# Where SBUF tiles lie: the same program with other start addresses

## The chip, the cores and the metric

The kernel runs on one core of a Trainium2 chip. The metric is the device time of one execution in microseconds. The kernel before was run three times: 2685.95, 2686.35 and 2686.78 us, median 2686.35.

## The reference

One layer over 2048 tokens of width 1024, float32. Both token mixers read the same normalised input, sigmoid gates merge them, and a two-level mixture of experts follows:

```
h    = rms_norm(x, g1)
qa, ka, va, qb, kb, vb, gates = split(h @ w_in)
ya   = swa_sink_attention(qa, ka, va)      # 8 query, 2 key heads, bands of 128 keys, bias, sinks
yb   = stick_breaking_attention(qb, kb, vb)  # 8 heads, strictly causal
       # A[t,s] = sig(z_ts) * prod_{s<j<t} (1 - sig(z_tj))
gate = sigmoid(gates + b_gate)
x    = x + (gate[0] * (ya @ w_proj_a) + gate[1] * (yb @ w_proj_b)) @ w_out
h2   = rms_norm(x, g2)
x    = x + moe(h2)   # top-1 of 4 groups, top-2 of its 8 experts: (silu(h2 @ w1) * (h2 @ w3)) @ w2
```

## The kernel before, in words

The program is written engine by engine; five functions run one after the other, each with its own SBUF tiles, and all engines meet at the end of each.

- `norm_and_values` (tiles nt_, 0 to 125 us): normalises and turns the rows, and makes the values of the second attention.
- `projection_and_banded_attention` (ip_, bb_, ba_, 125 to 520 us): the other projections, with the banded attention's steps set between them.
- `stick_breaking_and_gates` (sb_, 520 to 1284 us): 320 units of 128 query rows by up to 512 keys. For each unit TensorE makes the scores sb_z (two matmuls, L1097 and L1100), ScalarE two sigmoids (L945, L946), VectorE a running product into one of four rows of sb_R (L1018), GpSimd the product of sb_sig and sb_R (L1078). TensorE turns this into sb_pst (L1107), ScalarE and VectorE split it into sb_aT_hi and sb_aT_lo (L958, L1026), and TensorE multiplies with the values (L1124). The gate projections (sb_psg) are laid between by a fixed table of pace.
- `merge_and_output_projection` (mo_, 1284 to 1716 us): both attention projections, gates, output projection, second norm, logits.
- `routing_and_experts` (rt_, ex_, from 1716 us): the routing, a chain of small VectorE steps, then blocks of 128 rows. SP loads each expert's weights in pieces of 512 KB into ex_w; ScalarE rounds a piece (L1787, L1794), VectorE subtracts to get the rest (L1939, L1944).

Every float32 product is made of three passes over a rounded part and a rest, `_hi` and `_lo` (`passes3`, L50 to L54), so nearly all of TensorE's work stands on lines 52 to 54.

Tiles are taken with `nc.sbuf_tensor` under an `ExitStack`. The place that a tile gets within each partition follows from the order of these calls: each one takes the next free bytes, rounded up to a multiple of 32, above what is still held, and a function's tiles are given back when it ends. sb_R, [128, 4, 1025] float32, is 16400 bytes in a partition and is rounded up to 16416, the only large tile of its function that is no multiple of 64 bytes.

Of the kernel before, what the change touches and what calls it, by code (L numbers as in the profile page):

```python
# [18 lines left out]
I32 = mybir.dt.int32  # L19
# [4 lines left out]
P = 128  # L24
# [14 lines left out]
NE = 32  # L39
# [4 lines left out]
MAXB = 2 * S // P + NE  # L44
# [25 lines left out]
def norm_and_values(nc, x, g, ident_d, wv_d, hT_hi, hT_lo, vhl, stage, next_tiles, next_in, stored):  # L70

    with ExitStack() as c:
        sb = lambda n, s, d=F32: c.enter_context(nc.sbuf_tensor(n, s, d))
# [9 lines left out]
        junk = sb("nt_sq", [P, D], BF16)  # L83
        g_bc = sb("nt_g", [P, D])
        ident = sb("nt_ident", [P, P])
        wv = sb("nt_wv", [P, 2, 2, TC])
        wv_hi, wv_lo = sb("nt_wv_hi", [P, KD, TC], F32R), sb("nt_wv_lo", [P, KD, TC], F32R)
        vo = sb("nt_vo", [P, 2, HB, 2, HD], F32R)
        ssq, rms = sb("nt_ssq", [P, 2]), sb("nt_rms", [P, 2])
        eps, rstd = sb("nt_eps", [P, 1]), sb("nt_rstd", [P, 2])  # L90
        pt = c.enter_context(nc.psum_tensor("nt_ps", [P, 2, KD, P], F32))
        pv = c.enter_context(nc.psum_tensor("nt_pv", [P, 2, HB, HD], F32))
        g_in, ident_in = sem("nt_g_in"), sem("nt_ident_in")
# [167 lines left out]
def projection_and_banded_attention(nc, w_tiles, hT_hi, hT_lo, projF, qk_hi, qk_lo, hT_d, table, onehot, bias_z,  # L261
# [6 lines left out]
    KW = P + CHUNK  # L268
# [8 lines left out]
    with ExitStack() as c:  # L277
        sb = lambda n, s, d=F32: c.enter_context(nc.sbuf_tensor(n, s, d))
# [13 lines left out]
        tab_hi, pair = sb("bb_hi", [2 * NB, 8], F32R), sb("bb_pair", [2 * NB, 8], F32R)  # L292
        oh = sb("bb_onehot", [2 * NB, ZP], F32R)
        line = sb("bb_line", [8, ZP])
        sink = sb("ba_sink", [P, 2, 4])
        gq, gk = sb("ba_gq", [P, 1]), sb("ba_gk", [P, 1])
        eps, mx = sb("ba_eps", [P, 1]), sb("ba_mx", [P, 8])
        q = sb("ba_q", [P, 2, 4, P])
        k = sb("ba_k", [P, 2, KW])
        v = sb("ba_v", [P, 2, KW])  # L300
        qsq, rq, lnq = sb("ba_qsq", [P, 4, P]), sb("ba_rq", [P, 4, P]), sb("ba_lnq", [P, 4, P])
        kn, rk, ksq, lnk = sb("ba_kn", [P, KW]), sb("ba_rk", [P, KW]), sb("ba_ksq", [P, KW]), sb("ba_lnk", [P, KW])
        qn, vn = sb("ba_qn", [P, 2, 4, CHUNK]), sb("ba_vn", [P, 2, 2, P])
# [444 lines left out]
def stick_breaking_and_gates(nc, qk_hi, qk_lo, vhl, h0_hi, h0_lo, hT_d, w, w_in, wg_tiles, wg_d, b_gate, ident_d, neg_ident, mask_d,  # L748
# [48 lines left out]
    with ExitStack() as c:  # L797
        sb = lambda n, s, d=F32: c.enter_context(nc.sbuf_tensor(n, s, d))
        sem = lambda n: c.enter_context(nc.semaphore(n))
        qs, kh, kl = sb("sb_q", [P, 2, S], F32R), sb("sb_kh", [P, 2, S], F32R), sb("sb_kl", [P, 2, S], F32R)  # L800
        v = sb("sb_v", [P, 2, NT, P], F32R)
        sig = sb("sb_sig", [P, 5, TC])
        aT_hi, aT_lo = sb("sb_aT_hi", [P, 2, 4, TC], F32R), sb("sb_aT_lo", [P, 2, 4, TC], F32R)
        y, y2 = sb("sb_y", [HD, 2, TC]), sb("sb_y2", [HD, TC])
        zeros = sb("sb_zeros", [P, TC])
        ident = sb("sb_ident", [P, P])
# [2 lines left out]
        w_hi, w_lo = sb("sb_w_hi", [P, 2, KD, P], F32R), sb("sb_w_lo", [P, 2, KD, P], F32R)  # L809
        stage = sig[:, 4, 0:2 * P].rearrange("p (a s) -> p a s", a=2)  # L810
        go = sb("sb_go", [P, 2, TC])
        R = sb("sb_R", [P, 4, 2 * TC + 1])
        bias = sb("sb_bias", [P, NG])
        z = c.enter_context(nc.psum_tensor("sb_z", [P, 3, TC], F32))
        ps_t = c.enter_context(nc.psum_tensor("sb_pst", [P, 2, TC], F32))
# [15 lines left out]
        def unit(eng, s, j):  # L831
            if j >= 0:
                eng.wait_ge(s, j + 1)
# [172 lines left out]
        def _(dve):  # L1006
            def scan(j):
# [5 lines left out]
                if ch > g:  # L1013
                    unit(dve, scan_done, j - 4)
                    start = R[:, r, TC:TC + 1] if ch % 2 else R[:, r, 2 * TC:2 * TC + 1]
                    if ch % 2 == 0:
                        nc.vector.tensor_copy(R[:, r, 0:1], start)
                nc.vector.tensor_tensor_scan(R[:, r, first + 1:first + width + 1], z[:, j % 3, 0:width],  # L1018
                                             zeros[:, 0:width], start, ALU.mult, ALU.max).then_inc(scan_done, 1)
# [45 lines left out]
        def _(pool):  # L1065
# [8 lines left out]
            for j in range(NU):  # L1074
# [512 lines left out]
BT = MAXB + 3  # L1587


def routing_and_experts(nc, logits, cst, h2_d, h2_stored, w_pieces, ident_d, out, stage,  # L1590
                        w64, up_rounded, up_split):

    with ExitStack() as c:
        sb = lambda n, s, d=F32: c.enter_context(nc.sbuf_tensor(n, s, d))
        sem = lambda n: c.enter_context(nc.semaphore(n))
        HF, HK, QP = F // 2, KF // 2, KD // 2
        NR, NA, GA = GR + NE, 2 * NT, 8
        wr = sb("ex_w", [P, NPC, D])
        wu_hi, wu_lo = w64[:, 0, :, :], w64[:, 1, :, :]
        wd_hi, wd_lo = sb("ex_wd_hi", [P, 2, KF, D], F32R), sb("ex_wd_lo", [P, 2, KF, D], F32R)  # L1600
# [1 line left out]
        x_hi, x_lo = sb("ex_x_hi", [P, KD, P], F32R), sb("ex_x_lo", [P, KD, P], F32R)  # L1602
        s, g = sb("ex_s", [P, 2, HF]), sb("ex_g", [P, 2, HF])
        g_hi, g_lo = sb("ex_g_hi", [P, KF, P], F32R), sb("ex_g_lo", [P, KF, P], F32R)
        ident = sb("ex_ident", [P, P])
        idx_all, w_all = sb("idx_all", [P, BT], I32), sb("w_all", [P, MAXB + 1])
        blk_tab = sb("blk_tab", [1, 2 * NE], I32)
        w_rows = sb("ex_w_rows", [P, 1])
        ix_x, ix_y = sb("ex_ix_x", [P, 1], I32), sb("ex_ix_y", [P, 1], I32)
        O = sb("rt_O", [P, NT, NE], BF16)  # L1610
# [13 lines left out]
        gm, gk, gsum, gtop, mx0, mx1, ed, sd = (small[:, 320 + i * NT:320 + (i + 1) * NT] for i in range(8))  # L1624
        mx, tmp = [mx0, mx1], cst[:, C_TRI:C_TRI + 64]
# [447 lines left out]
def build(nc, x, g1, w_in, w_vb, w_gate, b_gate, g_q, g_k, sinks, table, wp, wo, g2, g2T, wr, b_all, w_exp,  # L2073
          ident, pair_ones, neg_ident, mask, onehot, cst_d, out):

    with ExitStack() as c:
# [15 lines left out]
        with ExitStack() as c0:  # L2092
            chunk = lambda n, where: where.enter_context(nc.sbuf_tensor(n, [P, KD, TC], F32R))
            h0_hi, h0_lo = chunk("h0_hi", c0), chunk("h0_lo", c0)
            with ExitStack() as c1:
                hT_hi = [h0_hi] + [chunk(f"h{t}_hi", c1) for t in range(1, NC_)]
                hT_lo = [h0_lo] + [chunk(f"h{t}_lo", c1) for t in range(1, NC_)]
                nt_sems = norm_and_values(nc, x, g1, ident, w_vb, hT_hi, hT_lo, vhl, stage, w_in, ip_w_in, vhl_stored)
                ip_sems = projection_and_banded_attention(nc, w_in, hT_hi, hT_lo, projF, qk_hi, qk_lo, hT_d, table, onehot,
                                                          bias_z, g_q, g_k, sinks, ident, pair_ones, yaT, nt_sems, stage,  # L2100
                                                          ip_w_in, w_gate, sb_w_in, vhl_stored, qk_stored, ya_stored)
            stick_breaking_and_gates(nc, qk_hi, qk_lo, vhl, h0_hi, h0_lo, hT_d, stage, sb_w_in, w_gate, wg_d, b_gate,
                                     ident, neg_ident, mask, ybT, gates, wp, yaT, mo_w_in, ip_sems, ya_stored, yb_stored, gates_stored)
# [89 lines left out]
```

## Time and profile before

| | |
|---|---|
| median of three runs | 2686.35 us |
| profiled execution: time, span | 2685.95 us, 2684.1 us |
| busy share: PE, weight loads, DVE, ACT, POOL | 96%, 80%, 61%, 56%, 23% |
| granted TensorE clock, mean | 0.983 |
| HBM traffic over the span | 199 GB/s |

The span is what the profiler saw from the first to the last instruction; 1.85 us of the profiled execution's time lie outside it. The engines' names are PE for TensorE, PEld for its weight loads, DVE for VectorE, ACT for ScalarE, POOL for GpSimd, SP for SyncE. A busy PE includes the pipeline of matmuls that overlap. L53 is line 53 of the program.

### The profile page before, as it was taken

To read this page: it belongs to the slowest core of one execution; us is meant where nothing else is said; L and a number is where in the kernel's file an instruction comes from. 1 tells how busy PE (TensorE), PEld (TensorE's weight loads), DVE (VectorE), ACT (ScalarE), POOL (GpSimd) and SP (SyncE) were. 2 spreads that over 40 slices of the span, in tenths; PEclk is the share of its full clock that TensorE was granted. 3 is DMA by queue.
4 is the path that set the end of the run, shared out by engine and by line. 5 is a ranking of instruction groups with operands and counts; after the bars stand their busy time and mean duration, and the time that the engine had idled before them with its cause. 6 is when DMAs were issued, how large, how long until landed. Compare 5 with 4: busy or idle time off the path is not lost. (4 is left out here: it accounts for less than half of the span.)

```text
span 2684.1 us, 41247 instructions
## 1 busy us (share of the span) xinstructions
PE 2586.1 (96%) x13573; PEld 2158.1 (80%) x13574; DVE 1638.4 (61%) x2216; ACT 1490.5 (56%) x2628; POOL 612.9 (23%) x707
## 2 busy tenths in 40 slices
PE   7999999989999999999899999699999999999997
PEld 6788777678888888888789998577788888888886
DVE  4400555478777777777543433588766677766673
ACT  4312777567767667676421211358666677766663
POOL 0000111144444444444000000022211222221221
PEclk9999999999999999999899999799999999999999
DMA  6454434586575556543644344479977789877782
GB/s 186 124 206 147 125 127 129 152 273 222 191 215 176 179 185 191 186 149 103 205 164 126 126 126 129 173 274 389 324 231 241 246 277 320 323 236 227 227 303 65
DMA packets 197344, 536.67 MB, mean 200 GB/s; under 512 B 20136, under 2 KB 70776, under 8 KB 192736
## 3 DMA queue, kind: packets, MB, share of 16 engines
q1 hardware_dynamic: 170576, 432.80, 47.1%
q0 software_dynamic: 26640, 102.18, 13.5%
q8 instruction: 78, 1.28, 0.2%
q14 instruction: 50, 0.41, 0.0%
HBM read 403.37 MB, written 131.53 MB: 199 GB/s over the span
## 5 line engine op out<-in xcount | busy, mean ns | idle before, releaser
L1078 POOL TENSOR_TENSOR sb_sig<-sb_sig,sb_R 128x512 f32<-128x512 f32 (+1 forms) x320 | 341.2, 1066 | 410.2 <-DVE sb_R L1018 409.9
L52 PE MATMUL ex_ps_h<-w_region,ex_x_hi 128*128 128x512 f32 x816 | 322.1, 395 | 0.8 <-DVE ex_x_lo L1934 0.8
L54 PE MATMUL ex_ps_h<-w_region,ex_x_lo 128*128 128x512 f32 x816 | 318.3, 390 | 0.0
L53 PE MATMUL ex_ps_h<-w_region,ex_x_hi 128*128 128x512 f32 x816 | 317.9, 390 | 0.0
L1939 DVE TENSOR_TENSOR w_region<-ex_w,w_region 128x1024 fp32r<-128x1024 f32 x248 | 284.7, 1215 | 1.4 <-ACT w_region L1787 1.3
L1018 DVE TENSOR_TENSOR_SCAN sb_R<-sb_z,sb_R,sb_zeros 128x512 f32<-128x512 f32 x192 | 245.6, 1279 | 57.8 <-ACT sb_z L946 57.6
L1944 DVE TENSOR_TENSOR ex_wd_lo<-ex_w,ex_wd_hi 128x1024 fp32r<-128x1024 f32 x200 | 239.3, 1218 | 40.8 <-ACT ex_wd_hi L1794 40.7
L1787 ACT CAST w_region<-ex_w 128x1024 fp32r<-128x1024 f32 x248 | 239.8, 1052 | 8.2 <-DMA ex_w<-in_w_exp 8.2
L958 ACT CAST sb_aT_hi<-sb_pst 128x512 fp32r<-128x512 f32 (+1 forms) x320 | 168.3, 526 | 134.1 <-PE sb_pst L1107 130.8
L1026 DVE TENSOR_TENSOR sb_aT_lo<-sb_pst,sb_aT_hi 128x512 fp32r<-128x512 f32 (+1 forms) x320 | 192.1, 601 | 51.9 <-ACT sb_aT_hi L958 49.8
L945 ACT ACTIVATE sb_sig<-sb_z 128x512 f32<-128x512 f32 (+1 forms) x320 | 172.4, 539 | 85.7 <-PE sb_z L1100 84.3
L1794 ACT CAST ex_wd_hi<-ex_w 128x1024 fp32r<-128x1024 f32 x196 | 196.5, 1057 | 3.7 <-DMA ex_w<-in_w_exp 3.7
L52 PE MATMUL ip_ps<-h_hi,ip_w_hi 128*128 128x512 f32 x448 | 182.8, 408 | 3.5 <-DVE ip_w_lo L605 3.5
L54 PEld LDWEIGHTS ex_ps_h<-w_region,ex_x_lo 128*128 128x128 f32 x816 | 153.2, 188 | 32.1
L52 PEld LDWEIGHTS ex_ps_h<-w_region,ex_x_hi 128*128 128x128 f32 x816 | 153.2, 188 | 31.3 <-issue 1.0
L53 PEld LDWEIGHTS ex_ps_h<-w_region,ex_x_hi 128*128 128x128 f32 x816 | 153.4, 188 | 30.5
L1107 PE MATMUL sb_pst<-sb_ident,sb_sig 128*128 128x128 f32 x1088 | 171.4, 273 | 6.7 <-DVE sb_aT_lo L1026 6.6
L54 PE MATMUL ip_ps<-h_hi,ip_w_lo 128*128 128x512 f32 x448 | 176.3, 393 | 0.0
L53 PE MATMUL ip_ps<-h_lo,ip_w_hi 128*128 128x512 f32 x448 | 176.0, 393 | 0.0
L1107 PEld LDWEIGHTS sb_pst<-sb_ident,sb_sig 128*128 128x128 f32 x1088 | 137.3, 140 | 45.9 <-issue 7.6
L946 ACT ACTIVATE sb_z<-sb_z 128x512 f32<-128x512 f32 (+1 forms) x320 | 171.4, 536 | 0.0
L1733 POOL DMA_INDIRECT out_x<-w_stage,ex_ix_y x52 | 83.8, 1612 | 380.4 <-ACT w_stage L1822 380.4
(296 smaller groups left out, 6164.4 us busy)
## 6 DMA issues: line engine op xcount, KB each, us to landing
ex_w<-in_w_exp SPq DMA_DIRECT2D x378, 512.0 KB, 9.3
sb_w_hi<-wg_d SPq DMA_DIRECT2D x48, 512.0 KB, 3.6
sb_w_lo<-wg_d SPq DMA_DIRECT2D x48, 512.0 KB, 4.5
gates<-sb_go SPq DMA_DIRECT2D x64, 256.0 KB, 4.0
mo_gates<-gates SPq DMA_DIRECT2D x64, 256.0 KB, 4.1
h<-w_stage POOLq DMA_DIRECT2D x17, 512.0 KB, 2.9
nt_x<-in_x SPq DMA_DIRECT2D x16, 512.0 KB, 4.1
vhl<-nt_vo SPq DMA_DIRECT2D x16, 512.0 KB, 5.1
```

Source lines behind the costliest of these rows:

```text
L52: nc.tensor.matmul(out, w_hi, x_hi, start=first, stop=False)
L53: nc.tensor.matmul(out, w_hi, x_lo, start=False, stop=False)
L54: return nc.tensor.matmul(out, w_lo, x_hi, start=False, stop=last)
L945: nc.scalar.activation(sig[:, j % 5, 0:width], z[:, j % 3, 0:width], ACT.Sigmoid, scale=HD ** -0.5)
L1018: nc.vector.tensor_tensor_scan(R[:, r, first + 1:first + width + 1], z[:, j % 3, 0:width], zeros[:, 0:width], start, ALU.mult, ALU.max).th ...
L1026: nc.vector.tensor_tensor(aT_lo[part], ps_t[:, j % 2, b0 * P:TC].rearrange("p (b s) -> p b s", s=P), aT_hi[part], ALU.subtract).then_inc(l ...
L1078: nc.gpsimd.tensor_tensor(sig[:, j % 5, 0:width], sig[:, j % 5, 0:width], R[:, r, first:first + width], ALU.mult).then_inc(a_done, 1)
L1107: last = nc.tensor.transpose(ps_t[:, j % 2, b * P:(b + 1) * P], sig[:, j % 5, b * P - OFF[j]:(b + 1) * P - OFF[j]], ident[:, :])
L1787: nc.scalar.copy(wu_hi[:, j, :], wr[:, j, :]).then_inc(up_rounded, 1)
L1794: nc.scalar.copy(wd_hi[:, u, k, :], wr[:, KD + k, :]).then_inc(down_rounded, 1)
L1939: nc.vector.tensor_tensor(wu_lo[:, j, :], wr[:, j, :], wu_hi[:, j, :], ALU.subtract).then_inc(up_split, 1)
L1944: nc.vector.tensor_tensor(wd_lo[:, u, k, :], wr[:, KD + k, :], wd_hi[:, u, k, :], ALU.subtract).then_inc(down_split, 1)
```

## The change

Calls of `sb(...)` are put in another order in four functions. No other line changes, and the built program has the same 16337 instructions in the same order on each engine with the same operands' shapes; the addresses in them differ.

```diff
@@ -83,11 +83,11 @@
         junk = sb("nt_sq", [P, D], BF16)
         g_bc = sb("nt_g", [P, D])
         ident = sb("nt_ident", [P, P])
+        ssq, rms = sb("nt_ssq", [P, 2]), sb("nt_rms", [P, 2])
+        eps, rstd = sb("nt_eps", [P, 1]), sb("nt_rstd", [P, 2])
         wv = sb("nt_wv", [P, 2, 2, TC])
         wv_hi, wv_lo = sb("nt_wv_hi", [P, KD, TC], F32R), sb("nt_wv_lo", [P, KD, TC], F32R)
         vo = sb("nt_vo", [P, 2, HB, 2, HD], F32R)
-        ssq, rms = sb("nt_ssq", [P, 2]), sb("nt_rms", [P, 2])
-        eps, rstd = sb("nt_eps", [P, 1]), sb("nt_rstd", [P, 2])
         pt = c.enter_context(nc.psum_tensor("nt_ps", [P, 2, KD, P], F32))
         pv = c.enter_context(nc.psum_tensor("nt_pv", [P, 2, HB, HD], F32))
         g_in, ident_in = sem("nt_g_in"), sem("nt_ident_in")
@@ -292,21 +292,23 @@
         tab_hi, pair = sb("bb_hi", [2 * NB, 8], F32R), sb("bb_pair", [2 * NB, 8], F32R)
         oh = sb("bb_onehot", [2 * NB, ZP], F32R)
         line = sb("bb_line", [8, ZP])
-        sink = sb("ba_sink", [P, 2, 4])
-        gq, gk = sb("ba_gq", [P, 1]), sb("ba_gk", [P, 1])
-        eps, mx = sb("ba_eps", [P, 1]), sb("ba_mx", [P, 8])
         q = sb("ba_q", [P, 2, 4, P])
         k = sb("ba_k", [P, 2, KW])
         v = sb("ba_v", [P, 2, KW])
-        qsq, rq, lnq = sb("ba_qsq", [P, 4, P]), sb("ba_rq", [P, 4, P]), sb("ba_lnq", [P, 4, P])
-        kn, rk, ksq, lnk = sb("ba_kn", [P, KW]), sb("ba_rk", [P, KW]), sb("ba_ksq", [P, KW]), sb("ba_lnk", [P, KW])
-        qn, vn = sb("ba_qn", [P, 2, 4, CHUNK]), sb("ba_vn", [P, 2, 2, P])
+        qsq, ksq = sb("ba_qsq", [P, 4, P]), sb("ba_ksq", [P, KW])
+        rq, rk = sb("ba_rq", [P, 4, P]), sb("ba_rk", [P, KW])
+        lnq, lnk = sb("ba_lnq", [P, 4, P]), sb("ba_lnk", [P, KW])
+        qn, kn = sb("ba_qn", [P, 2, 4, CHUNK]), sb("ba_kn", [P, KW])
+        vn = sb("ba_vn", [P, 2, 2, P])
         s = sb("ba_s", [P, 2, 2, 4, P])
         e = sb("ba_e", [P, 8, P])
         pT = sb("ba_pT", [P, 2, 4 * P])
         bias, bias_end = sb("ba_bias", [P, 4, P]), sb("ba_bias_end", [P, 4, P])
+        sink = sb("ba_sink", [P, 2, 4])
+        gq, gk = sb("ba_gq", [P, 1]), sb("ba_gk", [P, 1])
+        eps = sb("ba_eps", [P, 1])
         ident, ones = sb("ba_ident", [P, P]), sb("ba_ones", [P, P])
-        negm, sneg = sb("ba_negm", [P, 8]), sb("ba_sneg", [P, 8])
+        mx, negm, sneg = sb("ba_mx", [P, 8]), sb("ba_negm", [P, 8]), sb("ba_sneg", [P, 8])
         esink, rowsum = sb("ba_esink", [P, 8]), sb("ba_rowsum", [P, 8])
         den, rden = sb("ba_den", [P, 8]), sb("ba_rden", [P, 8])
         pb = lambda n, sh: c.enter_context(nc.psum_tensor(n, sh, F32))
@@ -800,6 +802,7 @@
         qs, kh, kl = sb("sb_q", [P, 2, S], F32R), sb("sb_kh", [P, 2, S], F32R), sb("sb_kl", [P, 2, S], F32R)
         v = sb("sb_v", [P, 2, NT, P], F32R)
         sig = sb("sb_sig", [P, 5, TC])
+        R = sb("sb_R", [P, 4, 2 * TC + 1])
         aT_hi, aT_lo = sb("sb_aT_hi", [P, 2, 4, TC], F32R), sb("sb_aT_lo", [P, 2, 4, TC], F32R)
         y, y2 = sb("sb_y", [HD, 2, TC]), sb("sb_y2", [HD, TC])
         zeros = sb("sb_zeros", [P, TC])
@@ -809,7 +812,6 @@
         w_hi, w_lo = sb("sb_w_hi", [P, 2, KD, P], F32R), sb("sb_w_lo", [P, 2, KD, P], F32R)
         stage = sig[:, 4, 0:2 * P].rearrange("p (a s) -> p a s", a=2)
         go = sb("sb_go", [P, 2, TC])
-        R = sb("sb_R", [P, 4, 2 * TC + 1])
         bias = sb("sb_bias", [P, NG])
         z = c.enter_context(nc.psum_tensor("sb_z", [P, 3, TC], F32))
         ps_t = c.enter_context(nc.psum_tensor("sb_pst", [P, 2, TC], F32))
@@ -1595,6 +1597,8 @@
         sem = lambda n: c.enter_context(nc.semaphore(n))
         HF, HK, QP = F // 2, KF // 2, KD // 2
         NR, NA, GA = GR + NE, 2 * NT, 8
+        idx_all, w_all = sb("idx_all", [P, BT], I32), sb("w_all", [P, MAXB + 1])
+        blk_tab, ident = sb("blk_tab", [1, 2 * NE], I32), sb("ex_ident", [P, P])
         wr = sb("ex_w", [P, NPC, D])
         wu_hi, wu_lo = w64[:, 0, :, :], w64[:, 1, :, :]
         wd_hi, wd_lo = sb("ex_wd_hi", [P, 2, KF, D], F32R), sb("ex_wd_lo", [P, 2, KF, D], F32R)
@@ -1602,9 +1606,6 @@
         x_hi, x_lo = sb("ex_x_hi", [P, KD, P], F32R), sb("ex_x_lo", [P, KD, P], F32R)
         s, g = sb("ex_s", [P, 2, HF]), sb("ex_g", [P, 2, HF])
         g_hi, g_lo = sb("ex_g_hi", [P, KF, P], F32R), sb("ex_g_lo", [P, KF, P], F32R)
-        ident = sb("ex_ident", [P, P])
-        idx_all, w_all = sb("idx_all", [P, BT], I32), sb("w_all", [P, MAXB + 1])
-        blk_tab = sb("blk_tab", [1, 2 * NE], I32)
         w_rows = sb("ex_w_rows", [P, 1])
         ix_x, ix_y = sb("ex_ix_x", [P, 1], I32), sb("ex_ix_y", [P, 1], I32)
         O = sb("rt_O", [P, NT, NE], BF16)
```

The starts within a partition, in bytes, as the two built programs have them:

| tile | before | after | moved by | over a multiple of 64: before, after | over 256: before, after |
|---|---|---|---|---|---|
| nt_wv (and nt_wv_hi, nt_wv_lo, nt_vo) | 178816 | 178944 | +128 | 0, 0 | 128, 0 |
| nt_ssq (and rms, eps, rstd) | 227968 | 178816 | -49152 | 0, 0 | 128, 128 |
| ba_q (k, v, qsq, vn, s, e, pT, bias alike) | 186496 | 186336 | -160 | 0, 32 | 128, 224 |
| ba_kn (rq, rk, ksq, lnq, lnk, qn: other shifts, same classes) | 199808 | 204000 | +4192 | 0, 32 | 128, 224 |
| ba_ident, ba_ones | 227456 | 227424 | -32 | 0, 32 | 128, 96 |
| ba_sink, gq, gk, eps | 186336 | 227296 | +40960 | 32, 32 | 224, 224 |
| sb_aT_hi (and aT_lo, y, y2, zeros, ident, nident, mask, hx, w_hi, w_lo, go) | 133248 | 149664 | +16416 | 0, 32 | 128, 160 |
| sb_R | 212096 | 133248 | -78848 | 0, 0 | 128, 128 |
| ex_w (and wd_hi, wd_lo, x_hi, x_lo, s, g, g_hi, g_lo) | 94432 | 95776 | +1344 | 32, 32 | 224, 32 |
| ex_ident | 225504 | 95264 | -130240 | 32, 32 | 224, 32 |
| idx_all (and w_all, blk_tab) | 226016 | 94432 | -131584 | 32, 32 | 224, 224 |

Not moved: w_stage (16512), the h tiles (h0_hi 24704, h0_lo 41088), nt_x (155776), the ip_ tiles (ip_w_hi 168064), sb_q, sb_kh, sb_kl, sb_v, sb_sig (123008), w_region (28896), every mo_ tile (mo_rows 209120) and all of PSUM and HBM.

## Rows read from the trace of the kernel before

**Rows 1.** The page: span, and busy time, share and instructions of each engine.
```profile
span 2684.1 us, 41247 instructions
...
PE 2586.1 (96%) x13573; PEld 2158.1 (80%) x13574; DVE 1638.4 (61%) x2216; ACT 1490.5 (56%) x2628; POOL 612.9 (23%) x707
```

**Rows 2.** Busy time by stage: start:end, length, busy (instructions) of each engine, granted clock, DMA share, GB/s.
```profile
520.00:1284.00 764.00, 753.25 (x4032) 622.38 (x4032) 566.70 (x774) 525.55 (x1088) 342.71 (x323) 0.99 0.60 188
1284.00:1716.00 432.00, 411.21 (x2688) 377.44 (x2688) 183.24 (x297) 102.65 (x169) 26.81 (x51) 0.98 0.46 147
1716.00:1757.00 41.00, 20.25 (x105) 17.94 (x106) 33.60 (x75) 11.18 (x14) 2.25 (x2) 0.55 0.48 180
1757.00:2684.00 927.00, 906.04 (x4284) 750.12 (x4284) 653.00 (x707) 598.12 (x751) 201.77 (x260) 0.99 0.78 265
```

**Rows 3.** Whom TensorE waited for: us in total, times, longest.
```profile
PE ex_ps_h L1993 <- DVE rt_O L1862: 12.7, 1, 12.7
...
PE nt_ps L238 <- DVE nt_h L196: 11.1, 3, 8.0
...
PE sb_pst L1107 <- DVE sb_aT_lo L1026: 6.6, 2, 4.7
...
PE ex_ps_g L2038 <- DVE ex_g L1954: 4.0, 6, 1.1
...
PE ex_ps_y L52 <- DVE ex_g_lo L1959: 2.9, 6, 1.9
```

**Rows 4.** Second pass (L53): count, least/median/greatest ns, first and last start, forms.
```profile
L53 PE MATMUL ex_ps_h<-w_region,ex_x_hi x816: 387/389/397, 1757.2 to 2662.8; 128*128 128x512 f32 x164
...
L53 PE MATMUL ip_ps<-h_lo,ip_w_hi x448: 387/389/628, 126.0 to 512.9; 128*128 128x512 f32 x150
...
L53 PEld LDWEIGHTS sb_psg<-h_lo,sb_w_hi x384: 187/188/331, 520.4 to 1280.2; 128*128 128x128 f32 x192
...
L53 PE MATMUL sb_psg<-h_lo,sb_w_hi x384: 387/389/628, 520.6 to 1280.4; 128*128 128x512 f32 x192
...
L53 PE MATMUL sb_psg<-sb_hx_lo,sb_w_hi x128: 387/393/398, 712.6 to 1094.9; 128*128 128x512 f32 x128
```

**Rows 5.** ScalarE's rounding of 1024 columns, by line (L446, L1787).
```profile
L446 ACT CAST ip_w_hi<-w_stage x13: 1042/1052/1065, 125.0 to 469.5; 128x1024 fp32r<-128x1024 f32 x13
...
L1787 ACT CAST w_region<-ex_w x248: 1042/1053/1062, 1775.3 to 2638.1; 128x1024 fp32r<-128x1024 f32 x124
```

**Rows 6.** VectorE's subtraction of 1024 columns, by line (L547, L1409).
```profile
L547 DVE TENSOR_TENSOR ip_w_lo<-w_stage,ip_w_hi x13: 1224/1225/1226, 126.1 to 470.6; 128x1024 fp32r<-128x1024 f32 x13
...
L1409 DVE TENSOR_TENSOR w_region<-w_stage,w_region x4: 1225/1226/1226, 1294.7 to 1309.5; 128x1024 fp32r<-128x1024 f32 x4
...
L1409 DVE TENSOR_TENSOR w_region<-mo_rows,w_region x3: 1225/1225/1226, 1292.0 to 1313.2; 128x1024 fp32r<-128x1024 f32 x3
```

**Rows 7.** GpSimd in order of time: start us, us, instruction, [idle before it].
```profile
800.29 1.30 POOL L1078 TENSOR_TENSOR sb_sig<-sb_sig,sb_R 128x512 f32<-128x512 f32 x1 [2.23 <-DVE sb_R L1018]
802.90 1.09 POOL L1078 TENSOR_TENSOR sb_sig<-sb_sig,sb_R 128x512 f32<-128x512 f32 x1 [1.31 <-DVE sb_R L1018]
804.99 1.09 POOL L1078 TENSOR_TENSOR sb_sig<-sb_sig,sb_R 128x512 f32<-128x512 f32 x1 [1.00 <-DVE sb_R L1018]
807.57 1.29 POOL L1078 TENSOR_TENSOR sb_sig<-sb_sig,sb_R 128x512 f32<-128x512 f32 x1 [1.48 <-DVE sb_R L1018]
...
812.33 0.87 POOL L1078 TENSOR_TENSOR sb_sig<-sb_sig,sb_R 128x384 f32<-128x384 f32 x1 [1.10 <-DVE sb_R L1018]
814.20 0.64 POOL L1078 TENSOR_TENSOR sb_sig<-sb_sig,sb_R 128x256 f32<-128x256 f32 x1 [1.00 <-DVE sb_R L1018]
```

**Rows 8.** Issue to landing: ex_w's loads (L1690), then nt_x's (L106).
```profile
DMA to landing us min/median/max: 3.4/9.5/16.6
...
DMA to landing us min/median/max: 3.4/4.1/8.5
```

**Rows 9.** DMA issues: out<-in, queue, count, KB each, median us to landing.
```profile
h<-w_stage POOLq DMA_DIRECT2D x17, 512.0 KB, 2.9
...
out_x<-mo_rows POOLq DMA_DIRECT2D x16, 512.0 KB, 2.9
```


## The prediction

> **What bounds the kernel now.** I read the page's first lines, then busy time by stage, then who TensorE waited for, and only then single lines. TensorE is busy 2586.1 of 2684.1 us [rows 1], and the reader should see in the table by stage that it is so in the three long ones: 753.25 of 764 us in stick breaking, 411.21 of 432 in the merge, 906.04 of 927 in the experts; only in the routing it is 20.25 of 41 us [rows 2]. All its idle time is 98.0 us. The longest named waits are 12.7 us for a chain of short VectorE steps in the routing and 11.1 us for the first normalised rows; 6.6 us in stick breaking are waits for sb_aT_lo [rows 3]. So a time can change here in two ways: a TensorE instruction itself gets longer or shorter, or one of the chains behind these 98 us does.
>
> **What the change is.** No instruction, wait, transfer, shape or order changes. What changes is the byte in each partition at which tiles start. I sort the moves by what stays the same. Every moved tile shifts by a multiple of 32 bytes. In nt_ and in the expert stage (1344 = 21 x 64) the place relative to 64 bytes stays as well. In ba_ and sb_ nearly all work tiles go from a multiple of 64 to 32 above one. sb_R moves by 78848 = 154 x 512 bytes and now follows sb_sig directly. A cost can therefore come only from: the 32-byte step in ba_ and sb_; the place relative to 256 bytes (224 becomes 32 in the experts, 128 becomes 160 in sb_); or which tiles are neighbours. The trace of before holds both kinds of start relative to 64 bytes side by side, so their cost can be read from it.
>
> **TensorE, 32-byte step.** All tiles of nt_, ip_ and sb_ that TensorE reads start at a multiple of 64 now, all of mo_ and of the experts 32 above one. The same matmul of 128x512 with the same weight load takes 389 ns in ip_ps, in sb_psg from h and in the experts' ex_ps_h; the weight load in sb_psg 188 ns; only sb_psg from sb_hx has 393, with the same ends of 387 and 398 [rows 4]. Both kinds of start give one number, so 3392 instructions (4032 of the stage [rows 2] less 640 score matmuls, two for each of 320 units, which read tiles that don't move) x 0 ns = 0 us. The bound is the spread inside the rows: from 389 to 393 or to 398 on the slow side, and 2 ns down to 387 on the fast one. I take 0, because the 32-byte start alone never goes with a different median. If it did matter nothing would hide it.
>
> **ScalarE and VectorE.** The 128x1024 rounding takes 1052 ns from w_stage to ip_w_hi (multiples of 64) and 1053 in the experts (32 above) [rows 5]. The subtraction takes 1225 ns in ip_, and 1225 and 1226 in mo_ (32 above) [rows 6]. Neighbours can be read too: mo_rows starts 44 x 4096 bytes behind w_region, while w_stage lies at no multiple of 4096 from w_region; 1225 against 1226 ns. After the change ex_w loses its distance of 16 x 4096 from w_region, and these rows say that this costs nothing. The ranges from least to greatest are wider, 1042 to 1065 ns for the rounding, so I allow 1.5%. Applied to all 98.0 us in which TensorE idles, as if all of it were such work, this bounds the term at 1.5 us either way; the value is 0.
>
> **GpSimd, the one place where the trace shows an address.** Four multiplies in a row read the four rows of sb_R, which start 0, 4, 8 and 12 bytes past a multiple of 16. They take 1.30, 1.09, 1.09 and 1.29 us [rows 7]. That is a difference of 0.2 us by four bytes. So I asked what the edit leaves of it. The narrower ones also start 512 bytes further into their row (384 wide, second row) or 1024 (256 wide, third row), and take 0.87 and 0.64 us [rows 7]: steps of 0.22 and 0.23 us for 128 columns, on one line with 1.09. Steps of 512 bytes thus do nothing, and sb_R moves by 154 of them while sb_sig stays. The pattern should come back as it is: 0 us. Even if all the wide multiplies went to the slow or to the fast value, GpSimd idled 1.0 to 2.2 us before each of them waiting for the scan [rows 7], and among the long waits of TensorE none is for it [rows 3].
> The Trainium skill, "SBUF — State Buffer", section "SBUF: two separate sides", states lines of 16 bytes, with full bandwidth only where successive accesses stay in one. By that rule too the edit does nothing, since each move is a multiple of 16; the 0.2 us by four bytes fit it as to size of step, though the page does not predict which of the four are slow.
>
> **Transfers.** Relative to 256 bytes the trace has only two kinds of start with such rows: 224 (ex_w, mo_rows) and 128 (nt_x, w_stage). The loads of ex_w and of nt_x land in 3.4 us at best, both [rows 8]. The stores of 512 KB from mo_rows and from w_stage have a median of 2.9 us, both [rows 9]. The new kinds, 32, 160 and 0, are not there. I take 0 for them too, since the step from 128 to 224 shows nothing. The bound is one reading step, 0.1 of 2.9 us or 3%, on the part of TensorE's 98.0 us that ends with a transfer; were it half of them, 1.7 us, but its longest waits all end with VectorE [rows 3], so I take a tenth, 0.3 us.
> The Trainium skill, "DMA: Bandwidth & Descriptors", section "How a descriptor splits into AXI transactions", speaks otherwise: a descriptor that does not start at a multiple of 256 bytes pays for the bytes below its start. Worked out from it as an estimate, a row of 4096 bytes costs 135 beats at 224, 129 at 32, 132 at 128 and 133 at 160: ex_w would be 4% cheaper and the sb_ tiles 1% dearer. The rows named show no such difference at their resolution.
>
> **The sum.** The profiled execution is 2684.1 us of span and 2685.95 us of time, so 1.85 us lie outside. 2685.95 + 0 (TensorE) + 0 (ScalarE, VectorE) + 0 (GpSimd) + 0 (DMA) = 2685.95; the median of the runs is 0.4 us above that execution, so 2686.3. Added bounds of the small terms: 1.5 + 0.3 us, which gives 2684.5 to 2688.1.
>
> **Rivals.**
> Slower, by TensorE's reads in stick breaking. Mechanism: tiles that start 32 bytes above a multiple of 64 (aT, ident, hx, w_hi, w_lo) are read or loaded more slowly while ScalarE, VectorE and GpSimd write next to them. In the mo_ and expert stages GpSimd does no wide elementwise work, so the even numbers there don't exclude it altogether; the 393 ns of sb_hx is the row that speaks for a disturbance in just this stage [rows 4]. Price: 3392 x 4 ns = 13.6 us, 2699.9; at 398 ns, 3392 x 9 = 30.5 us, 2716.8. The idle 10.8 us of the stage [rows 2] hide none of it: they are waits of TensorE, which longer instructions would follow all the same. It decides from 5.4 / 3392 = 1.6 ns an instruction. Against it: the medians of both kinds of start are the same to a nanosecond with ScalarE and VectorE at work in both.
> Faster, by the experts' loads. Mechanism: ex_w's rows start 32 instead of 224 bytes above a multiple of 256, their loads get shorter, and the waits at the start of that stage go. For it: half of these loads take 9.5 us or more to landing [rows 8], in a stage where the DMA engines are 0.78 busy [rows 2]. Price: at most what TensorE waited there, 4.0 + 2.9 = 6.9 us [rows 3], so 2679.4. Against: the waits named are for ex_g and ex_g_lo, neither of them a weight tile, and the best landing is as good as elsewhere. This is the case in which the page on DMA would be right.
> That the edit moves nothing is not a rival: the placement is fixed when the program is built, and the table of starts shows the moves.
>
> **How the numbers follow.** About 0.2%, 5.4 us, is what a measurement of this kernel can tell from no change. No change 0.88: matmuls, roundings and subtractions show one duration at both kinds of start relative to 64 bytes. Slower rival 0.08, since its one condition (three engines beside TensorE) stands nowhere in the trace with the other start. Faster rival 0.04. The 8 in 10 lie inside the forecast's own case; I widen its 2684.5 to 2688.1 by about half a microsecond for chance between executions and lean to the slow side: 2684.0 to 2689.3.
>
> **What would show it.** In the profile after: weight loads at 188 and 128x512 matmuls at 389 ns in sb_psg; multiplies again 1.3, 1.1, 1.1, 1.3; the row of 520 to 1284 us with TensorE at 753; waits of the same names within a microsecond. Wrong, if sb_psg's or sb_pst's instructions are longer, or if the expert stage ends earlier with the named 6.9 us gone.

## The result, and the profile after

The changed kernel takes 2703.49 us (median of 4 runs, 2700.03 to 2704.55) against 2686.15 us of the kernel before: ratio 1.0061, interval 1.0048 to 1.0074. It is slower by 17 us. The forecast was no change, 2686.3 us with 2684.0 to 2689.3, and 0.08 for slower.

Span and busy times, from the page of the changed kernel:

```profile
span 2703.7 us, 41246 instructions
...
PE 2608.2 (96%) x13572; PEld 2159.8 (80%) x13574; DVE 1642.1 (61%) x2216; ACT 1489.6 (55%) x2628; POOL 612.8 (23%) x707
```

Against [rows 1] the span is 19.6 us longer and TensorE's busy time 22.1 us, with the same instructions (one record more or less is missing from a trace); VectorE, ScalarE and GpSimd differ by 4, 1 and 0 us. The profiled execution took 2705.57 us, 2 us above the median, so 19.6 us of span stand for the 17 us of the medians. The loss is inside TensorE's own instructions. Where it lies, by stage, each from the first TensorE instruction of one stage to that of the next, nt_ from the span's start and the experts to the end of TensorE's last instruction (worked out from the instructions' starts in each profile, us):

| kernel | nt_ | ip_ and ba_ | sb_ | mo_ | routing | experts |
|---|---|---|---|---|---|---|
| before | 125.3 | 394.9 | 766.4 | 439.3 | 30.8 | 913.2 |
| after | 128.2 | 393.2 | 770.3 | 441.4 | 31.1 | 925.2 |

Twelve of the 19.6 us are in the experts, four in stick breaking, three in nt_, two in the merge, and the projections are 1.7 us shorter. One profile of each kernel doesn't show all of these: in the profiles of the experiments below in which a stage's own tiles keep their starts, nt_ takes 125.3 to 127.9 us, stick breaking 764.6 to 766.7 and the merge 438.0 to 441.6. The experts and stick breaking lie clear of such differences, nt_ hardly and the merge not.

TensorE's clock is not the reason. The granted clock is 0.99 in the experts [rows 2], and in the same stage of the changed kernel

```profile
1764.00:2703.00 939.00, 922.89 (x4284) 750.70 (x4284) 656.77 (x709) 597.43 (x751) 202.12 (x260) 0.99 0.77 262
```

The second pass of TensorE's products in the changed kernel (count, least/median/greatest ns), which answers to [rows 4]:

```profile
L53 PE MATMUL ex_ps_h<-w_region,ex_x_hi x816: 392/394/629, 1765.0 to 2682.4; 128*128 128x512 f32 x164
...
L53 PE MATMUL ip_ps<-h_lo,ip_w_hi x448: 387/389/628, 128.6 to 514.1; 128*128 128x512 f32 x150
...
L53 PEld LDWEIGHTS sb_psg<-h_lo,sb_w_hi x384: 187/188/334, 521.6 to 1285.3; 128*128 128x128 f32 x192
...
L53 PE MATMUL sb_psg<-h_lo,sb_w_hi x384: 389/396/632, 521.9 to 1285.5; 128*128 128x512 f32 x192
...
L53 PE MATMUL nt_pv<-nt_wv_lo,h_hi x128: 390/393/628, 14.1 to 124.1; 128*128 128x512 f32 x128
...
L53 PE MATMUL sb_psg<-sb_hx_lo,sb_w_hi x128: 387/393/398, 715.1 to 1098.8; 128*128 128x512 f32 x128
```

ex_ps_h went from 389 to 394 ns, sb_psg from h from 389 to 396, while ip_ps and sb_psg from sb_hx kept 389 and 393, and the weight load 188 ns. nt_pv is new here; in the kernel before it was

```profile
L53 PE MATMUL nt_pv<-nt_wv_lo,h_hi x128: 387/389/628, 14.3 to 121.2; 128*128 128x512 f32 x128
```

that is 389 against 393. Since matmuls overlap, what counts is the time from one start to the next. TensorE in order of time in the kernel before, then in the changed kernel (start us, us, instruction):

```profile
1999.97 0.39 PE L52 MATMUL ex_ps_h<-w_region,ex_x_hi 128*128 128x512 f32 x1
2000.19 0.39 PE L53 MATMUL ex_ps_h<-w_region,ex_x_hi 128*128 128x512 f32 x1
2000.42 0.39 PE L54 MATMUL ex_ps_h<-w_region,ex_x_lo 128*128 128x512 f32 x1
2000.65 0.39 PE L52 MATMUL ex_ps_h<-w_region,ex_x_hi 128*128 128x512 f32 x1
```

```profile
2009.98 0.39 PE L52 MATMUL ex_ps_h<-w_region,ex_x_hi 128*128 128x512 f32 x1
2010.22 0.39 PE L53 MATMUL ex_ps_h<-w_region,ex_x_hi 128*128 128x512 f32 x1
2010.45 0.39 PE L54 MATMUL ex_ps_h<-w_region,ex_x_lo 128*128 128x512 f32 x1
2010.68 0.39 PE L52 MATMUL ex_ps_h<-w_region,ex_x_hi 128*128 128x512 f32 x1
```

Three steps take 0.68 us before and 0.70 after. Over all 816 matmuls of each pass the median time from start to start is 227 ns before and 233 after. I call this the pace. It is the main part of the experts' 12.0 us: 3 x 816 x 6 ns = 14.7 us, of which the two waits at the end of the next view give 5.1 back. With every start taken up to the next one, the count closes: the two passes with x_hi take 11.0 us more, the pass with x_lo, behind which most of those waits lie, 1.3 us more, and all the rest of the stage 0.3 us less. The waits:

```profile
PE ex_ps_h L1994 <- DVE rt_O L1863: 13.3, 1, 13.3
...
PE nt_ps L238 <- DVE nt_h L196: 11.4, 3, 7.9
...
PE ex_ps_g L2039 <- DVE ex_g L1955: 1.4, 2, 0.7
...
PE ex_ps_y L52 <- DVE ex_g_lo L1960: 0.4, 2, 0.2
```

The last two rows were 4.0 and 2.9 us in [rows 3]. That a slower TensorE meets them less fits, but their size is partly chance: together they take 1.8 to 5.9 us in the six profiles (this one and five below) whose ex_ps_h is slower, and 4.4 to 7.8 in the eight others. The other parts of the prediction can be checked at once. The four multiplies of GpSimd [rows 7]:

```profile
803.09 1.30 POOL L1080 TENSOR_TENSOR sb_sig<-sb_sig,sb_R 128x512 f32<-128x512 f32 x1 [2.22 <-DVE sb_R L1020]
805.71 1.10 POOL L1080 TENSOR_TENSOR sb_sig<-sb_sig,sb_R 128x512 f32<-128x512 f32 x1 [1.32 <-DVE sb_R L1020]
807.81 1.09 POOL L1080 TENSOR_TENSOR sb_sig<-sb_sig,sb_R 128x512 f32<-128x512 f32 x1 [1.00 <-DVE sb_R L1020]
810.46 1.29 POOL L1080 TENSOR_TENSOR sb_sig<-sb_sig,sb_R 128x512 f32<-128x512 f32 x1 [1.56 <-DVE sb_R L1020]
```

and the roundings and the subtraction [rows 5, 6]:

```profile
L448 ACT CAST ip_w_hi<-w_stage x13: 1043/1050/1063, 127.9 to 470.8; 128x1024 fp32r<-128x1024 f32 x13
...
L1788 ACT CAST w_region<-ex_w x248: 1039/1049/1056, 1781.5 to 2657.1; 128x1024 fp32r<-128x1024 f32 x124
...
L549 DVE TENSOR_TENSOR ip_w_lo<-w_stage,ip_w_hi x13: 1225/1226/1227, 129.0 to 471.9; 128x1024 fp32r<-128x1024 f32 x13
```

1050 and 1049 ns against 1052 and 1053, 1226 against 1225, though ex_w changed its place over 256 bytes and against w_region. These terms were 0 as forecast.

### The profile page after: what moved, and what is told of

Its sections match the earlier page's. It is cut to its first block and busy times, and to the rows that moved or that the text cites. A ratio compares the mean times of both kernels' runs of the same rounds, so it can differ in the third digit from the quotient of the medians.

```text
span 2703.7 us, 41246 instructions
## 1 busy us (share of the span) xinstructions
PE 2608.2 (96%) x13572; PEld 2159.8 (80%) x13574; DVE 1642.1 (61%) x2216; ACT 1489.6 (55%) x2628; POOL 612.8 (23%) x707
## 5 line engine op out<-in xcount | busy, mean ns | idle before, releaser
L52 PE MATMUL ex_ps_h<-w_region,ex_x_hi 128*128 128x512 f32 x816 | 327.0, 401 | 0.8 <-DVE ex_x_lo L1935 0.8
L53 PE MATMUL ex_ps_h<-w_region,ex_x_hi 128*128 128x512 f32 x816 | 322.4, 395 | 0.0
L1788 ACT CAST w_region<-ex_w 128x1024 fp32r<-128x1024 f32 x248 | 239.3, 1049 | 7.9 <-DMA ex_w<-in_w_exp 7.1
L53 PEld LDWEIGHTS ex_ps_h<-w_region,ex_x_hi 128*128 128x128 f32 x816 | 153.5, 188 | 35.0
L53 PE MATMUL ip_ps<-h_lo,ip_w_hi 128*128 128x512 f32 x448 | 175.5, 392 | 0.0
```

The source lines that it names most:

```text
L52: nc.tensor.matmul(out, w_hi, x_hi, start=first, stop=False)
L53: nc.tensor.matmul(out, w_hi, x_lo, start=False, stop=False)
L1788: nc.scalar.copy(wu_hi[:, j, :], wr[:, j, :]).then_inc(up_rounded, 1)
```

## The experiments

The kernels differ only in the order in which tiles are taken. Each product has two instructions in the trace: LDWEIGHTS loads 128x128 of one tile, the weights, and MATMUL streams up to 512 columns of another past them. The names behind the arrow are first the streamed tile, then the weights' tile. "Distance" is the start of the weights' tile minus the start of the streamed one: ex_x against w_region, h against nt_wv, sb_w against h, sb_v against sb_aT, w_region (which holds the merge's weights) against mo_y. In the kernel before all of these are multiples of 512 bytes. The change made them 320, -128, 32, -32 and left the last at 0; sb_w against sb_hx kept its distance, since both moved, and ip_ps's and ex_g's against their tiles too. That sorts the rows above into slower and equal, hence the theory ("pair theory" in the expectations). I made it after seeing these rows, so it needed kernels of its own. Its rivals: the start of x by itself ("place theory"), ex_w against w_region, that is ScalarE's, VectorE's and the transfers' work beside TensorE ("writers theory"), and the prediction's own rival of the 32-byte step.

**The expert stage alone, and the rest alone.** The two hunks of the diff apart.

```diff
 # ex_only: only this
+        idx_all, w_all = ...; blk_tab, ident = ...
         wr = sb("ex_w", [P, NPC, D])
```

> The kernel before with the new order of tiles in the expert stage alone: x_hi and x_lo lie 181568 bytes (320 over a multiple of 512) behind w_region instead of 180224 (352 x 512); ex_w, wd, g move with them. Pair theory (a matmul's pace depends on the distance between the tile it streams and the tile whose weights load beside it, modulo 512): matmuls of ex_ps_h start every 233 ns instead of 227, 2448 of them, so +14.5 us, 2700.5 us; nt_pv and sb_psg as before at 227 and 230. Place theory (the start of x alone over 256, 32 instead of 224): the same here. Writers theory (ex_w against w_region, ScalarE and VectorE beside TensorE): the same here. The prediction's rival by the 32-byte step in stick breaking: about 2686 us, no loss.

Measured 2698.44 us, ratio 1.0045 (1.0028 to 1.0062); experts 926.8 us, stick breaking 765.1, nt_ 126.9. Its rows of the second pass:

```profile
L53 PE MATMUL ex_ps_h<-w_region,ex_x_hi x816: 392/394/628, 1755.6 to 2674.6; 128*128 128x512 f32 x164
...
L53 PE MATMUL sb_psg<-h_lo,sb_w_hi x384: 387/389/628, 521.2 to 1279.4; 128*128 128x512 f32 x192
...
L53 PE MATMUL nt_pv<-nt_wv_lo,h_hi x128: 387/389/628, 14.2 to 122.9; 128*128 128x512 f32 x128
```

```diff
 # rest_only: the first three functions as in the changed kernel, the experts as before
```

> The complement: new order in the first three functions, the expert stage as before. Pair theory: nt_pv every 232 ns (nt_wv_hi is 128 over a multiple of 512 behind h0), sb_psg from h +3 ns (distance 32 over), sb_psg from sb_hx unchanged since both moved, sb_psy +2 ns; 384 x 5.5 + 1152 x 2.5 + 640 x 2 ns = 6 us at most, 2689 to 2692 us; ex_ps_h at 227. Rival by the 32-byte step in stick breaking: all of the loss, 2703 us, sb_hx as slow as h.

Measured 2689.90 us, ratio 1.0013 (1.0003 to 1.0022); experts 913.5, stick breaking 769.8, nt_ 126.4 us. Its rows:

```profile
L53 PE MATMUL ex_ps_h<-w_region,ex_x_hi x816: 387/389/396, 1761.7 to 2667.7; 128*128 128x512 f32 x164
...
L53 PE MATMUL sb_psg<-h_lo,sb_w_hi x384: 389/396/628, 520.3 to 1283.3; 128*128 128x512 f32 x192
...
L53 PE MATMUL nt_pv<-nt_wv_lo,h_hi x128: 390/393/628, 14.1 to 122.3; 128*128 128x512 f32 x128
...
L53 PE MATMUL sb_psg<-sb_hx_lo,sb_w_hi x128: 387/393/398, 712.9 to 1096.6; 128*128 128x512 f32 x128
```

12.5 + 3.9 = 16.4 of the 17.3 us: the parts add up within the runs' noise, and three quarters come from the experts. That rules out the 32-byte step in stick breaking as the cause: the experts' tiles kept their place over 64 bytes, and sb_hx and sb_w, which both took the step, pair at 393 ns as before, while sb_w with the unmoved h went to 396.

**The streamed tile instead of the weights.**

```diff
 # w_moved: the changed kernel, and
-        logits, cst, b_bc = sb("logits", ...), sb("rt_cst", [P, CW], F32), sb("rt_bias", ...)
+        logits, b_bc = sb("logits", ...), sb("rt_bias", ...)
         w64 = sb("w_region", [P, 2, KD, D], F32R)
+        cst = sb("rt_cst", [P, CW], F32)
```

> The changed kernel with rt_cst behind w_region, so that w_region starts 1728 bytes lower while x_hi stays where the change put it (32 over a multiple of 256): the distance is 183296 = 358 x 512 again. Pair theory: ex_ps_h back at 227 ns (-14.5 us), but mo_ps_m, whose weights are in w_region and whose mo_y does not move (distance 192 over), gets slower by up to 6 ns x 1536 = 9 us; 2694 to 2699 us. Place theory: ex_ps_h stays at 233, about 2703 us. Writers theory: ex_w lies at a multiple of 4096 less 64 x 16 from w_region again (0 over 512), so it too says 227 for ex_ps_h, but nothing for mo_ps_m.

Measured 2686.56 us, ratio 1.0004 (0.9995 to 1.0014). Its rows:

```profile
L53 PE MATMUL ex_ps_h<-w_region,ex_x_hi x816: 387/389/401, 1759.1 to 2667.3; 128*128 128x512 f32 x164
...
L53 PE MATMUL mo_ps_m<-mo_y_lo,w_region x512: 276/281/420, 1291.6 to 1666.6; 128*128 128x256 f32 x171
```

ex_ps_h is back at 389 ns (pace 227) with x exactly where the change put it: the place theory falls. The total came out at the time of before and not at the expected 2694 to 2699 us, because two things cancel: stick breaking keeps its loss (770.2 us), and the merge is shorter (436.3 against 439.3). One part of my expectation fell too: mo_ps_m did not get slower but faster, from

```profile
L53 PE MATMUL mo_ps_m<-mo_y_lo,w_region x512: 278/283/420, 1287.1 to 1665.2; 128*128 128x256 f32 x171
```

283 to 281 ns, pace 120 to 117.5. Its distance is 64 over 256 now (I had given the opposite sign, 192), and its matmuls stream 256 columns, not 512. Multiples of 256 are thus not the best distance for every width. Here only w_region moved, so for the merge its own place and the distance are not told apart.

**x alone, all but x, and a control.**

```diff
 # x_plus_320: s, g, g_hi, g_lo before x; then 320 bytes of other small tiles, then x
+        s, g = ...; g_hi, g_lo = ...; tri, w_rows, ix_x = ...
         x_hi, x_lo = sb("ex_x_hi", ...), sb("ex_x_lo", ...)
 # x512: the same with ex_ident (512 bytes) in the place of the 320
 # ex_all_1536: idx_all, w_all, blk_tab, ident (1344 bytes) before ex_w; s, g, g_hi, g_lo (8192)
 #   and rt_w, w_rows, ix_x (192) before x
```

> The kernel before, in which only x_hi and x_lo change their place over 512 (320 more); ex_w, wd, g, w_region keep theirs. Pair theory and place theory: ex_ps_h at 233 ns, 2700.5 us. Writers theory: 227 ns, 2686 us, since ex_w and w_region lie as before.

Measured 2698.98 us, ratio 1.0043 (1.0027 to 1.0060):

```profile
L53 PE MATMUL ex_ps_h<-w_region,ex_x_hi x816: 391/396/398, 1758.6 to 2677.5; 128*128 128x512 f32 x164
```

> Control for the reordering itself: the same order of tiles as in the kernels that shift x, but with 512 bytes between, so x lies at a multiple of 512 from w_region. Pair theory with a unit of 512 or less: 227 ns, 2686 us. If the unit is larger (the distance before was 180224 = 11 x 16384, now 188928, an odd multiple of 512): 233 ns, 2700 us.

Measured 2687.49 us, ratio 1.0003 (0.9993 to 1.0013):

```profile
L53 PE MATMUL ex_ps_h<-w_region,ex_x_hi x816: 387/389/628, 1759.8 to 2664.9; 128*128 128x512 f32 x164
```

> All the expert stage's tiles are moved: ex_w, wd, s and g by 1344 and more, x_hi and x_lo by 9728 = 19 x 512, so that x lies at a multiple of 512 from w_region while ex_w is 320 over. Pair theory: ex_ps_h at 227 ns, time as before, 2686 us. Writers theory (ex_w against w_region): 233 ns, 2700 us.

Measured 2689.17 us, ratio 1.0015 (1.0006 to 1.0025):

```profile
L53 PE MATMUL ex_ps_h<-w_region,ex_x_hi x816: 387/389/628, 1758.8 to 2665.6; 128*128 128x512 f32 x164
```

Moving x by 8192 + 320 bytes makes the whole loss of the experts (926.4 us), with ex_w and w_region where they were; 8192 + 512 bytes do nothing (912.8 us); and with ex_w 320 off but x at a multiple of 512 the matmuls are at 389 again. The writers theory falls for the large part. A small one is left: ex_all_1536 is 0.15% slower than before, and its experts take 914.6 us against 913.2, which does not account for all of it. In all fourteen kernels the median pace of the x_hi passes goes by the distance: 227 ns in the eight where it is a multiple of 256, 231 to 235 in the six others.

**Which distances.** Orders as above with other small tiles between, and in nt_ with ssq, rms and eps (32 bytes each) ahead of nt_wv.

```diff
 # x256_nt64, x128_nt32, x32_nt96, x192_sb64: the numbers are bytes ahead of x and ahead of nt_wv;
 # sb64: sb_bias (64 bytes) ahead of sb_aT
```

> x 256 over a multiple of 512 from w_region, nt_wv 64 over from h0. If the unit of the pair theory is 512 bytes: ex_ps_h at 232 to 233 ns, 2701 us; if it is 256 bytes: 227 ns, 2686 us (the distances measured so far, 320 and 128, are no multiple of 256 either). nt_pv between 228 and 232.

Measured 2687.51 us, ratio 1.0004 (0.9994 to 1.0014):

```profile
L53 PE MATMUL ex_ps_h<-w_region,ex_x_hi x816: 387/389/396, 1758.6 to 2664.5; 128*128 128x512 f32 x164
...
L53 PE MATMUL nt_pv<-nt_wv_lo,h_hi x128: 388/388/632, 14.2 to 123.2; 128*128 128x512 f32 x128
```

> Two distances in two stages: x 128 over a multiple of 512 from w_region, nt_wv 32 over from h0. Pair theory: ex_ps_h every 232 to 233 ns as nt_pv was at 128 in the changed kernel; nt_pv about 3 ns over 227 as sb_psg was at 32. About 2701 us. If the size of the distance sets the loss in proportion, ex_ps_h is at 229 to 230 and nt_pv at 227 to 228.

Measured 2697.64 us, ratio 1.0046 (1.0030 to 1.0062):

```profile
L53 PE MATMUL ex_ps_h<-w_region,ex_x_hi x816: 390/393/404, 1756.6 to 2676.7; 128*128 128x512 f32 x164
...
L53 PE MATMUL nt_pv<-nt_wv_lo,h_hi x128: 391/394/632, 14.0 to 123.1; 128*128 128x512 f32 x128
```

> x - w_region 32 over 256; h0 - nt_wv_hi 160 over 256 (that is -96). Pair theory: ex_ps_h 3 to 7 ns over 227, since sb_psg lost 3 at 32 and nt_pv 6 at -32: 2693 to 2703 us; nt_pv between 229 (its value at -64) and 232 (at -128). Proportion theory (loss grows with distance from the nearest multiple of 256): ex_ps_h at 228 to 229, 2688 to 2691 us.

Measured 2702.99 us, ratio 1.0060 (1.0042 to 1.0078):

```profile
L53 PE MATMUL ex_ps_h<-w_region,ex_x_hi x816: 392/395/628, 1760.7 to 2679.8; 128*128 128x512 f32 x164
...
L53 PE MATMUL nt_pv<-nt_wv_lo,h_hi x128: 388/394/628, 14.0 to 125.5; 128*128 128x512 f32 x128
```

> x - w_region 192 over 256, that is -64, the distance at which nt_pv took 229 ns, while at +64 ex_ps_h took 233 to 235. If only the signed distance counts, ex_ps_h is at 229: about 2691 us from this part; if the stage counts too, 232 to 235. In stick breaking sb_w - h is 64 over and sb_v - sb_aT is -64, and sb_R lies 64 bytes further from sb_sig: sb_psg from h 3 to 5 ns slower than 230, sb_psg from sb_hx unchanged, sb_psy within 2 ns of 230; GpSimd's four multiplies still 1.29, 1.09, 1.09, 1.29 us (only 4-byte steps under 16 count), otherwise another pattern. 2692 to 2703 us together.

Measured 2694.56 us, ratio 1.0033 (1.0023 to 1.0043); its second pass, and GpSimd in order of time:

```profile
L53 PE MATMUL ex_ps_h<-w_region,ex_x_hi x816: 387/394/628, 1759.4 to 2669.9; 128*128 128x512 f32 x164
...
L53 PE MATMUL sb_psg<-h_lo,sb_w_hi x384: 388/394/628, 521.3 to 1282.3; 128*128 128x512 f32 x192
```

```profile
800.12 1.30 POOL L1078 TENSOR_TENSOR sb_sig<-sb_sig,sb_R 128x512 f32<-128x512 f32 x1 [2.24 <-DVE sb_R L1018]
802.72 1.10 POOL L1078 TENSOR_TENSOR sb_sig<-sb_sig,sb_R 128x512 f32<-128x512 f32 x1 [1.30 <-DVE sb_R L1018]
804.81 1.10 POOL L1078 TENSOR_TENSOR sb_sig<-sb_sig,sb_R 128x512 f32<-128x512 f32 x1 [1.00 <-DVE sb_R L1018]
807.46 1.29 POOL L1078 TENSOR_TENSOR sb_sig<-sb_sig,sb_R 128x512 f32<-128x512 f32 x1 [1.55 <-DVE sb_R L1018]
```

The unit is 256 bytes: 256 and 512 give 389 ns. The loss is not in proportion: 32 bytes cost as much as 128. Mean pace, ns over that at distance 0, of the second pass in nt_pv (base 227.0 to 228.9 in kernels that leave it) and of the x_hi passes in ex_ps_h (base 229.9), by distance over 256:

| distance | 32 | 64 | 128 | 160 | 192 | 224 |
|---|---|---|---|---|---|---|
| ex_ps_h | 5.8 | 6.0 to 6.3 | 5.6 | | 2.7 | |
| nt_pv | | | 3 to 5 | 3 to 5 | 0 to 2 | 4 to 6 |

Each entry but 64 of ex_ps_h and 128 of nt_pv is from one profile, and the passes differ: the x_lo pass loses nothing at 192 (227.5 ns against 227.9), and the third pass of nt_pv loses 7 to 9 ns at 160 (237.1). At 192 (64 below a multiple of 256) both stages lose least.

The transposes, which stream 128 columns, show no distance at all. ex_ps_x (weights from w_stage, ex_ident streamed) has a distance of 160 over 256 in the kernel before and of 96, 32, 128 and 224 in the changed kernel, x128_nt32, x32_nt96 and x192_sb64, and a median pace of 109 ns in each; sb_pst keeps 108 ns at 0, 224 and 192. sb_R 64 bytes further from sb_sig left GpSimd's 1.30, 1.10, 1.10, 1.29 us in place: only steps of 4 bytes within 16 have shown an effect.

**A faster one?** Keep ex's distance and take 64 for the merge.

```diff
 # mo64: rt_cst behind w_region as in w_moved, x with w_rows and ix_x (64 bytes) ahead; the rest as before
 # w_ex: rt_cst behind w_region, and the expert stage in the new order; the rest as before
```

> The kernel before with w_region 1728 bytes lower and x 9984 bytes higher (both tiles moved by other amounts; x_hi now starts 32 over a multiple of 256 as in the changed kernel), so that x - w_region is 0 over 256 again and w_region - mo_y is 64 over 256. Pair theory with a unit of 256 bytes, distance counted from the streamed tile to the weights: ex_ps_h at 227 ns in spite of all moves, and mo_ps_m at the pace of w_moved (117 to 118 ns where the kernel before has 120; 1536 x 3 = 4.6 us less), nt_, sb_ as before: 2681.5 us, faster than both. Place theory (start of x over 256): ex_ps_h at 233, 2696 us or more. If the gain of w_moved in mo_ps_m came from something else that the changed kernel has: 2686 us.

Measured 2686.83 us, ratio 1.0000 (0.9991 to 1.0009):

```profile
L53 PE MATMUL ex_ps_h<-w_region,ex_x_hi x816: 387/389/395, 1752.8 to 2663.4; 128*128 128x512 f32 x164
...
L53 PE MATMUL mo_ps_m<-mo_y_lo,w_region x512: 276/281/416, 1286.5 to 1660.3; 128*128 128x256 f32 x171
```

> The kernel before with the new order of the expert stage's tiles and rt_cst behind w_region. Every tile of the expert stage has moved, yet x - w_region (183296) and ex_w - w_region (68608) are both multiples of 512, and w_region - mo_y is 64 over 256 as in w_moved and mo64. Pair theory: ex_ps_h at 227 ns although x starts where it starts in the changed kernel; mo_ps_m at 117 to 118 ns; the expert stage 913 to 916 us where mo64, whose ex_w - w_region is 192 over 512, had 918; stick breaking 765 to 766. Together 2681 to 2683 us, 0.1 to 0.2% under the kernel before. Place theory: ex_ps_h at 233 and 2694 us or more.

Measured 2683.76 us, ratio 0.9994 (0.9985 to 1.0003):

```profile
L53 PE MATMUL ex_ps_h<-w_region,ex_x_hi x816: 387/389/628, 1752.9 to 2659.5; 128*128 128x512 f32 x164
...
L53 PE MATMUL mo_ps_m<-mo_y_lo,w_region x512: 276/281/415, 1287.0 to 1660.2; 128*128 128x256 f32 x171
```

The merge gets what was expected in both: 435.1 and 434.4 us against 439.3. The total of mo64, expected at 2681.5 us, was a miss: it loses the gain again in the experts (918.1 us), w_ex does not (914.3). 3.0 of mo64's 4.9 us lie on ex_ps_y, whose own distance is 0 over 256 in both kernels, so the pair theory doesn't explain them. In mo64 ex_w starts 67264 bytes from w_region, 192 over a multiple of 256, in w_ex at a multiple of 512. A small writers' part would fit mo64 and ex_all_1536; against it, ex_only and x_plus_320 have ex_w at 64 and at 0 over 256 and experts of 926.8 and 926.4 us. It stays open. w_ex's median is 2 us under the kernel before, and its interval holds 1: I can't call it faster. The expected range of 2681 to 2683 us missed it by 1 us.

## Why the prediction was wrong

- The step that failed stands in "What the change is": "A cost can therefore come only from: the 32-byte step in ba_ and sb_; the place relative to 256 bytes ...; or which tiles are neighbours." I sorted tiles one by one, by their own start. The prediction named the place over 256 bytes, but priced it for the transfers alone, so the experts' matmuls had no term at all. A matmul and the weight load beside it read two tiles, and what counts is the distance between those two. The table of starts held it: 180224 = 352 x 512 before, 181568 after.
- "TensorE, 32-byte step": the rows were read rightly and each number came back, but they could not carry "x 0 ns = 0 us". The experts start 32 bytes above a multiple of 64, ip_ and sb_ do not, yet all of them are alike in distance (0 over 512). A comparison of groups that agree in the deciding quantity says nothing about it. In place of 0 us for TensorE the runs showed 3.9 us by the first three functions and 12.5 by the experts, each alone, and 17.3 with both. The bound from inside the rows, 4 to 9 ns, had the right size by luck, since it came from the spread and not from this cause: 5 to 6 ns were found. One reading was off without weight: w_stage, which TensorE reads in the merge and the experts, starts at a multiple of 64 and not 32 above one.
- The slower rival had the sign and nearly the size (13.6 us, 2699.9) but the wrong place and reason: stick breaking got 3.9 us, the experts 12.0. That its price came near is luck. Tiles that took the 32-byte step together lost nothing. Its chance of 0.08 rested on that reason. The honest unknown was larger: each tile that TensorE reads had been moved, against others that had not.
- GpSimd, ScalarE, VectorE: 0 as forecast; the reasoning over steps of 512 bytes for sb_R held, and the experiment with 64 bytes extends it.
- Transfers: nothing speaks against the term of 0. ex_w's median time to landing fell, as the Trainium skill, "DMA: Bandwidth & Descriptors", section "How a descriptor splits into AXI transactions", would have it for a start at 32 instead of 224 if its rule on bytes that are fetched holds for bytes that are written too. It went from 9.3 us to

```profile
ex_w<-in_w_exp SPq DMA_DIRECT2D x378, 512.0 KB, 7.8
```

but in x_plus_320, where ex_w did not move, it is 7.9 us too. What sets this median is not shown: it is 3.5 us in x32_nt96 and 10.0 in x512, both with ex_w in its old place. The packets themselves answer the rule: those of 4096 bytes on SP's queue in the experts (1790 to 2600 us) take 159 ns in the median and 167.4 in the mean, both with ex_w at 224 before and at 32 after. The 4% are not there.
- The faster rival's waits did shrink, 6.9 to 1.8 us, a third of the 14.7 us, but not by its mechanism: the packets got no shorter, and in x_plus_320, where ex_w stayed, they are 4.9 us.

## What to carry to other kernels

Treat the distance between the streamed tile and the weights' tile as part of a kernel: before tiles are reordered or a small one is slipped in, list weights start minus streamed start over 256 bytes for each product, and keep it; this case says so for 512 streamed columns, while 256 columns did better at 64 and 128 showed nothing. When a trace is to show that a quantity has no effect, look first whether its groups differ in anything else that the edit changes; relations between operands are such a thing.

## What the runs showed of the hardware

- 128x512 float32 matmuls with a 128x128 weight load each start every 227 ns (228 to 232 in stick breaking) when the two tiles lie a multiple of 256 bytes apart, and every 231 to 237 ns at 32, 64, 128, 160 or 224 over it; at 192 it is 226 to 232 by pass. The weight load's own duration stays at 187 to 188 ns. With 256 streamed columns a pace of 117.5 ns goes with a distance of 64, and 120 with 0; with 128 columns it is 108 to 109 ns at every distance seen.
- Moving x by 8512 bytes, 320 over a multiple of 512, with w_region and ex_w in place, changed the pace by 6 ns; moving it by 8704 changed nothing. The Trainium skill, "TensorE: Matmul & The Clock Gate", section "Step-by-step: what each phase is for", says that weights and streamed operand have a read port each and that loading the next weights takes nothing from the running matmul. These runs don't agree, 227 against 233 ns: something in the two reads depends on their distance. That the two meet in the memory would fit; it was not seen directly, and no run tells how.
- GpSimd's two-input multiply of 128x512 takes 1.30 or 1.29 us with one input 0 or 12 bytes past a multiple of 16 and 1.09 or 1.10 at 4 or 8; moving that input by 64 bytes or by 154 x 512 left this as it was.
